# Transposes of the decayed queries and of the normalised retention rows by DMA instead of by TensorE

## The reference

```
xm = rmsnorm(x) * (1 + sc) + sh                       # adaLN from c
h, bg, cg, za, q, k, v, zb, ga, gb = split(xm @ w_in) # q, k rotated; 8 heads, dk 64, dv 128
scores = (q k^T) * decay mask                         # per chunk of 128 tokens
ret    = scores @ v + (q * q_dec) @ state             # forward and backward state
rn     = per-head normalisation of ret, * gn_w
y_b    = (silu(zb) * rn) @ w_b
y_a    = (silu(za) * bg * conv3(cg * h)) @ w_a
x      = rmsnorm(x + g * ((sigmoid(ga) * y_a + sigmoid(gb) * y_b) @ w_out))
```

## Time and profile before

| | |
|---|---|
| median of 3 runs | 927.28 us (925.75 to 927.38) |
| the profiled execution | 927.01 us, span 925.5 us on its slowest core |
| spans of the 8 cores | 918.7 to 925.5 us |
| granted TensorE clock, mean | 0.984 to 0.989 of full speed |
| TensorE busy | 826.9 us, 89% |
| VectorE, ScalarE, GpSimd busy | 443.5, 383.8, 320.3 us |
| DMA queue of POOL (software) | 5904 packets, 31.46 MB, 20.4% of the DMA engines' time |
| DMA queue of SP (hardware) | 17446 packets, 39.20 MB, 13.4% |

### The profile page before, as it was taken

The page is one execution under the profiler, slowest core; times in us unless marked ns, Lnnn a source line. Parts: engine busy times, 40 slices in busy tenths (PEclk is TensorE's granted clock), DMA queues, the critical chain, the costliest instruction groups (busy, mean ns, idle before and its releaser), DMA issues.

```text
span 925.5 us, 14783 instructions; the slowest of 8 cores (918.7 to 925.5 us)
## 1 busy us (share of the span) xinstructions
PE 826.9 (89%) x4856; PEld 405.0 (44%) x4856; DVE 443.5 (48%) x1053; ACT 383.8 (41%) x674; POOL 320.3 (35%) x341
## 2 busy tenths in 40 slices
PE   0385999989977899999988999999999999999995
PEld 0242445545534454444544444444444444444442
DVE  1177624656757665756633244433454512244435
ACT  0496756777556545555543212221222211222212
POOL 1053523555466444444420032112223243233331
PEclk9997999999999899999999999999999999999998
DMA  9994701950065000000402090543106070035143
GB/s 139 229 275 113 154 30 59 170 166 7 4 101 102 3 8 7 4 7 7 86 4 44 16 165 2 92 91 59 33 1 137 1 180 2 1 115 160 69 114 136
DMA packets 23425, 71.60 MB, mean 77 GB/s; under 512 B 2859, under 2 KB 9131, under 8 KB 21686
## 3 DMA queue, kind: packets, MB, share of 16 engines
q0 software_dynamic: 5904, 31.46, 20.4%
q1 hardware_dynamic: 17446, 39.20, 13.4%
HBM read 93.72 MB, written 8.39 MB: 110 GB/s over the span
## 4 chain that ended last, share of the span: by engine, by line
PE 73%; ACT 7%; DMA 7%; DVE 7%; issue 4%; POOL 2%; DVEq 0%; ACTq 0%; POOLq 0%; SPq 0%
PE P L961 51%; PE P L549 10%; PE P L1226 6%; DMA st<-ada_w 4%; DMA kz<-x 3%; ACT tm L944 2%; DVE vb L976 2%; PE P L657 1%; DVE xmt L464 1%; PE P L910 1%; DVE tm L796 1%; ACT st L869 1%; DVE tm L536 1%; ACT vb L435 1%; PE P L911 1%
## 5 line engine op out<-in xcount | busy, mean ns | idle before, releaser
L961 PE MATMUL P<-xmt,vb 128*128 128x512 bf16 x1280 | 283.1, 379 | 2.7 <-DVE wt L1125 1.8
L961 PEld LDWEIGHTS P<-xmt,vb 128*128 128x128 bf16 x1280 | 124.5, 98 | 152.3 <-issue 3.6
L549 PE MATMUL P<-wt,xmt 128*128 128x512 bf16 x688 | 163.9, 391 | 15.4 <-DVE xmt L464 9.6
L961 PE MATMUL P<-xmt,wt 128*128 128x512 bf16 x512 | 121.1, 385 | 3.8 <-ACT tm L944 2.0
L549 PEld LDWEIGHTS P<-wt,xmt 128*128 128x128 bf16 x688 | 65.8, 100 | 94.4 <-issue 25.2
L1128 POOL TENSOR_TENSOR kz<-tm,wt 128x1024 bf16<-128x1024 f32 x16 | 45.7, 2856 | 161.3 <-DVE wt L1125 161.3
L961 PEld LDWEIGHTS P<-xmt,wt 128*128 128x128 bf16 x512 | 49.3, 99 | 59.0 <-issue 8.1
L1205 DVE SCALAR_TENSOR_TENSOR tm<-tm,P 128x512 f32<-128x512 f32 x32 | 22.0, 688 | 87.5 <-PE P L961 87.5
L1207 POOL TENSOR_TENSOR st<-st,tm 128x512 bf16<-128x512 bf16 x32 | 39.8, 1244 | 65.8 <-DVE tm L1205 65.8
L961 PE MATMUL P<-vb,wt 128*128 128x512 bf16 x256 | 58.8, 379 | 4.1 <-DVE vb L976 4.1
L1081 DVE TENSOR_TENSOR wt<-P,wt 128x512 f32<-128x512 f32 x32 | 22.1, 692 | 82.0 <-ACT wt L1080 62.1
(11 more groups left out here) (160 smaller groups left out, 1141.7 us busy)
## 6 DMA issues: line engine op xcount, KB each, us to landing
kz<-x SPq DMA_DIRECT2D x24, 512.0 KB, 8.6
wt<-x SPq DMA_DIRECT2D x24, 512.0 KB, 4.4
vb<-w_conv POOLq DMA_DIRECT2D x16, 512.0 KB, 9.9
out<-wt SPq DMA_DIRECT2D x15, 512.0 KB, 3.0
st<-ada_w POOLq DMA_DIRECT2D x4, 1024.0 KB, 20.6
vb<-w_mix POOLq DMA_DIRECT2D x8, 512.0 KB, 10.7
cm<-rope SPq DMA_DIRECT2D x33, 64.0 KB, 3.4
wt<-w_v POOLq DMA_DIRECT2D x4, 512.0 KB, 7.3
```

What stands on the lines that cost most here:

```text
L549: ins = e.matmul(pf(bank)[:, 0:wid], lhsT=lhs_x(ch, k), rhs=w[:, k, c0_:c0_ + wid], start=(k == 0), stop=(k == 7))
L961: ins = e.matmul(pf(bank), lhsT=lhs(k), rhs=rhs(k), start=(k == 0), stop=(k == 7))
```

## The change

Both pairs of eight TensorE transposes and an ACT copy become one DMA each, `dma_start_transpose`, issued from SP at the same place of the loop: `qfb` to `qdT[n % 2]` in `r_qtp`, and `retn` to `vb[:, n]` in `r_rtp`. Each moves 128 x 1024 elements of bf16, 256 KB, from SBUF to SBUF. PSUM bank 0 and the identity are no longer used in the loop. The rest of the program is as it was.

```diff
         def r_qtp(n):
             i = 1 if n == 0 else 0
 
-            def f_qdtp(e):
-                ins = None
-                for h in range(8):
-                    ins = e.transpose(out=pb(0)[:, h * 128:(h + 1) * 128], in_=qfb[i][:, h, :], identity=identb)
-                return ins
-            P.op("pe", f_qdtp, reads=[f"qfb{i}", "identb"], writes=["P0"])
-            P.op("act", lambda e: e.activation(out=qdT[n % 2], in_=pb(0).rearrange("p (a b) -> p a b", a=8), func=AF.Copy),
-                 reads=["P0"], writes=[f"qdT{n % 2}"])
+            P.dma("sp", lambda e: e.dma_start_transpose(out=qdT[n % 2], in_=qfb[i].rearrange("p a b -> p (a b)")),
+                  f"tq{n % 2}", reads=[f"qfb{i}"], writes=[f"qdT{n % 2}"])
@@
         def r_rtp(n):
-            def f_rtp(e):
-                ins = None
-                for c in range(8):
-                    ins = e.transpose(out=pb(0)[:, c * 128:(c + 1) * 128], in_=retn[:, c * 128:(c + 1) * 128], identity=identb)
-                return ins
-            P.op("pe", f_rtp, reads=["retn", "identb"], writes=["P0"])
-            P.op("act", lambda e: e.activation(out=vb[:, n, :], in_=pb(0), func=AF.Copy), reads=["P0"], writes=[f"v{n}"])
+            P.dma("sp", lambda e: e.dma_start_transpose(out=vb[:, n, :].rearrange("p (a b) -> p a b", a=8), in_=retn),
+                  "tr", reads=["retn"], writes=[f"v{n}"])
```

## The result

The changed kernel takes 953.8 us (median of 4 runs), the kernel before 927.3: the ratio is 1.0278 with a 95% interval of 1.0251 to 1.0306. It is 26 us slower. The profiled execution took 954.2 us, its span 952.6 us on core 0. In some executions of every one of these programs a few cores run at a lower clock and the time is longer, so the ratios, and the medians in the table of experiments, leave such executions out (of the changed kernel one of four, and 953.4 us is the median of the rest).

What follows compares the result with a forecast made beforehand. TensorE, 73% of the chain that ended last, was taken as the bound in full chunks, a chain of dependent steps in chunks 0 to 3. 927.0 + 36.0 (early chunks) - 9.5 (full chunks) = 953.5 us, 8-in-10 range 924 to 1010.

Steps and rivals of the forecast that it cites:

- The collision with the weight loads: Chunk 1's query transpose lands only when the weights have, scores at 292.0 against 273.52: +18.5 us, chunk 0's 3.5 included.
- this one goes nearly alone: Chunk 0's query transpose, weight loads only just issued, is hardly delayed: first scores at 268.3 instead of 264.77.
- Chunks 2 to 4: Early chunks after the loads: period 12.3 us, together +8.2, besides terms for transposes delaying each other and for the clock.
- L: Time from a transpose's source being ready to its landing, taken as 5.5 us between 2.1 and 14.4.
- The term for one transpose held by the other: Early chunks: the retn transpose, issued first, holds the DMA engines 3.7 us, the query one comes 1.4 later, three times: +4.2.
- The clock: Early chunks: after longer gaps TensorE falls to 1.2 GHz, 1.7 us in each of three more chunks: +5.1 us.
- The full chunks: Later chunks where TensorE sets the pace: DMA hidden, 0.9 us gained each, less in b1's chunks: -9.5 us in sum.
- 6.8 us later, enough again: Chunks 4, 8 and 12: b1 starts 6.8 us after retn is ready, so the row transpose's landing stays hidden.
- The cover of 7.2 us: Full chunks: queries are ready 7.2 us before their scores once the transposes are gone, so a 5.5 us landing is hidden.
- the first rival: Transposes as cheap as stores and not held by the loads, landing in 2.3 us: 919 us, chance 0.13.
- The slow rival: Transposes limited by their small pieces, landing in 11 us, also in the full chunks: +108, 1035 us; chance 0.20.
- The break-even case: Landing near 4 us, little delay by the loads, early loss equal to the full chunks' gain: 927 us, chance 0.05.

Runs made afterwards that it cites:

- The run with the loads behind it: Changed kernel, but POOL issues the w_b and w_gb loads only once the first transpose has landed; 947.2 us, ratio 1.0213 to the kernel before.
- the added matmuls: Changed kernel without the two weight loads, plus twelve matmuls into unused PSUM bank 0 ahead of the scores of chunks 1 to 4; 921.7 us, one execution.
- The hybrid: Changed kernel with DMA transposes only for queries from chunk 5 and rows from chunk 3, earlier ones on TensorE and ScalarE; 920.1 us, ratio 0.9927 to the kernel before.

## Why the prediction came out right, point by point

The time was forecast as 953.5 and is 953.8. That it is so close is luck: two terms were off by 11 to 12 us, in opposite directions. The mechanism, a transpose held until the weights have landed and a chain of early chunks that pays for its latency, was right.

- **The collision with the weight loads** (+18.5 forecast, some 31 measured up to chunk 1's scores). The mechanism is shown: transposes land when the loads do. The step that failed is "this one goes nearly alone" about chunk 0. Issued 0.3 us behind the first load and 0.3 us ahead of the second, it was held for 29.7 us, and the hold that I gave to chunk 1 fell to chunk 0. As chunk 0 is followed by another full round of the chain before chunk 1's scores, this costs 12 us more. The run with the loads behind it gives the case that I had described, 947 us.
- **Chunks 2 to 4** (+17.5 forecast, 36.1 - 29.6 = 6.5 measured). L was mis-sized: 3.0 to 3.2 us from issue to landing, not 5.5. With that the working holds: 6.67 us to the next qfb and 3.3 us to the scores give 10.0, the length of these chunks at the full clock. Three of them are only 1.3 us longer than before; the other 5.2 of the 6.5 are the clock. The estimate from the number of packets, 3.5, was the good one, and no run shows the 2 us added for a scattered write. The term for one transpose held by the other, 1.4 us a chunk, is not there either, for two reasons: the two are issued 5 us apart here (306.52 and 311.57), not 2.25, and a transpose keeps the engines 1.4 us, not 3.7. The latter should have been worked out from the packets' time, not as what was left of L. In the four full chunks where they are issued 2.2 us apart the rows landed after 4.7, 3.0, 3.0 and 5.3 us, so something can hold the first of them there; no run tried what.
- **The clock** (1.7 us a chunk forecast, 1.6 to 1.9 measured by the added matmuls; +5.1 forecast, 5.2 measured). Right for the slowest core, though it now hit chunks 0 to 3 as well as 4, and once more in chunk 12; cores 1, 5, 6 and 7 were spared it in chunks 2 and 3. What decides that, no run shows.
- **The full chunks** (-9.5 forecast). 13.42 us for 14.31 is the 0.9 to the digit. From chunk 4 to chunk 15 the changed kernel makes up 5.9 us, since chunk 12 gave back 2.4; behind chunk 15 it makes up 3.1 more, of which 1.4 were expected; the rest is open. The step that failed here is "6.8 us later, enough again" about b1: it was read from chunk 4, but in the changed kernel's chunk 8 the rows are ready at 401.98 and b1 starts at 406.10, 4.1 us later, which covers a landing of 3.0 us and not one of 4.6 or 5.3. The hybrid, which has this term alone, is 7 us faster: right but for such a late b1 in chunk 8 and the collision of chunk 14 with the slab loads, which the prediction does not name.
- **The cover of 7.2 us** was a little large: in the changed kernel the queries of the chunk at 383.27 were ready at 376.52, 6.75 us ahead. 6.4 us are hidden, 9.8 are not.
- **The rivals.** The cheap transposes of the first rival are nearly there in the quiet stretches, 3.0 us beside a store of 2.1, but the loads are not all that keeps its 919 us from coming true: without them the changed kernel takes 928.3. The rest is the early chunks, above all their clock; the added matmuls bring it to 921.7 and the hybrid, which leaves these chunks alone, to 920.1. Of the two pages that the prediction set against each other the trace comes nearer to the Trainium skill's "Advanced Engine Details and Errata", section X-Bar Transpose, which calls transpose DMAs as fast as regular ones (3.0 against 2.1 us here), than to the 1309 ns for a 128x128 block in its "VectorE: DVE Perf Modes", section on the three transpose paths: eight blocks in one DMA landed in 3.0 us, not the estimated 10.5. The slow rival has fallen. The break-even case is the changed kernel without the loads, 928.3.

## What to carry to other kernels

Price a DMA that takes an engine's work by the time from its source to its consumer, stage by stage: the same 3 us were hidden and worth 0.9 us a chunk where TensorE was the bound, and lengthened every round where a chain was, with the lower clock on top. Look for every large load in flight when it is issued; beside POOL's converting loads even 64 KB waited for the end of 4 MB, and a transpose issued 0.3 us ahead of the second of them waited too. Where a loop has both kinds of stage, let the first chunks keep the low-latency path.

## What the runs showed of the hardware

A transposing DMA of 128 x 1024 bf16 from SBUF to SBUF took 1.23 us of SP to issue, 1056 packets, 1.4 us of the 16 DMA engines and 3.0 us to land, with 3.0 to 3.4 in 22 of the 32 on core 0 and 3.6 to 5.7 in nine. Beside the weight loads it took 29.7 us. SP can be held too while it issues: 4.53 us for the query transpose beside the slabs, and 15.22 us for one of rows beside the weights in the run with the loads behind the first transpose.

The packets fit a simple picture that no run tested. The two weight loads are 288 packets, 18 on each engine, of 1.4 us each (55.5% of 16 x 45 us); a transpose is 66. If an engine took one packet of either queue in turn, no more than 18 of the 66 would pass while the loads last, and the other 48 would need an estimated 1.0 us more, at 21 ns each. The first transpose landed 0.8 us after w_gb.

Behind waits of about 3 us TensorE's granted clock was at its lower level in all early chunks on some cores and at the full one in chunks 2 and 3 on others; with twelve matmuls in each wait it was full there on all eight.
